# Second block's attention: two heads' scores and values on halves of TensorE, with two buffers for turned weights

## The chip, the cores and the metric

One Trainium2 chip; the kernel is one launch on one of its cores. The metric is the time of an execution in microseconds (us), the median of several runs. The core's engines are TensorE (matrix multiply; PE in profiles), ScalarE (ACT), VectorE (DVE), GpSimd (POOL) and SyncE (SP, which only issues transfers). They meet through semaphores: each engine runs its own list of instructions in order, and an instruction waits until named counters have reached a value.

## The reference, cut to what matters

A first block (two layers) and then a second block (two layers) over x of 256 tokens by 1024. A layer of the second block computes two attentions of 8 heads each, "mla" with keys of 96 features and "dilated" with keys of 64, both with values of 64:

```
for l in range(DEPTH):                       # DEPTH = 2
    h = rmsnorm(x, attn_norm[l])
    c_q, c_kv, k_r, q_d, k_d, v_d = split(h @ w_in[l])
    o_a = mla_mixer(c_q, c_kv, k_r, ...)     # 8 heads, q.k over 96, softmax, times v (64)
    o_b = dilated_attention(rmsnorm(q_d), rmsnorm(k_d), v_d, rel_bias)   # 8 heads, q.k over 64, + bias
    x = x + concat(o_a, o_b) @ w_out[l]
    x = x + conv_ffn(rmsnorm(x, ffn_norm[l]), ...)
```

Everything is float32. A head has 256 queries and 256 keys.

## The kernel before

Activations lie with features on partitions and the 256 tokens along the free axis. Weights come from HBM in pieces of at most 128 x 2048 (`raw`, three buffers) and are split into a rounded half (`wh`, made by ScalarE) and the rest (`wl`, VectorE), so that a large product is three fast float32r matmuls. The small products of attention are plain float32; each such matmul shows as two records in the trace.

A planner, `plan_program`, writes one list of steps, and each engine walks this list and issues its own part of every step. The order of the list is thus the order on every engine at once. PSUM has 8 banks, handed out in the order in which they were given back; `E2` are two buffers for a head's scores and weights, `pT2` one buffer for turned weights, `tmp` eight scratch buffers.

In a layer of the second block the order comes from generators. `mla_proj` is the list of projection work (pieces of `w_in`, the queries, four key parts, the values); `heads("d")` and `heads("m")` are the attention of the eight dilated and the eight mla heads. The dilated heads are interleaved with `mla_proj`, the mla heads with what is left of it and with half of the output projection (`dil_half`). `run_pending` issues at once what an earlier piece left to do: the norm and rotation of a head group (step `hn2`: TensorE sums of squares and a rotation by matmul, ScalarE a logarithm and an exponential, VectorE up to four products over 96 x 512), of which `queries` leaves two.

A head h goes through these steps: `sc2` (scores S: two matmuls into a bank), `exp2` (E: VectorE adds the bias for dilated heads and takes the maximum, ScalarE the exponential), `wt2` (W: VectorE divides), `turn2` (T: four transposes by TensorE, then ScalarE copies the bank to `pT`), `val2` (V: two matmuls; after every odd head ScalarE and VectorE write the pair's result as `hc_hi` and `hc_lo`). Before, the loop's turn for h is E(h+1), W(h), S(h+2), some projection work, V(h-1), T(h). Scores of an odd head use rows 64 to 127 of the array for dilated heads (rows 0 to 95 for mla heads whatever the head), and its values go to columns 64 to 127, that of an even head to 0 to 63.

In the rows below `kd,qd` are dilated scores, `k,q` mla scores, `cst,e` transposes, `pT,vd` and `pT,v` values of dilated and mla heads, `96*96 96x512` the matmuls of `hn2` for the queries, `ckn_hi,wh` key parts, `raw,csil` a product of the first block (step `mod`) in which four matmuls use four groups of 32 columns.

Of the kernel before, what the change touches and what calls it, by code (L numbers as in the profile page):

```python
# [15 lines left out]
P = 128  # L16
# [138 lines left out]
class Memory:  # L155
    def __init__(self, nc, banks):
# [219 lines left out]
def plan_program(M, pieces):  # L376
# [153 lines left out]
    def run_pending():  # L530
        while pending:
            pending.pop(0)()
# [486 lines left out]

    E2, pT2 = Bufs(M.E2), Bufs(M.pT2)  # L1020
    s = "x"
    for l in range(2):
# [90 lines left out]
        def mla_values(f):  # L1113
            for j in range(2):
# [4 lines left out]
                v_toks.append(x)  # L1119

        def mla_proj():
            for fn in (lambda: dil_piece(1), lambda: dil_piece(3), lambda: queries(0), lambda: dil_piece(5),
                       lambda: queries(1)):
                run_pending()
                tk = fn()
                if tk is not None:
                    hfree["x"] = [tk]
                yield
            f = take(("ukv", l))
            prev = None  # L1130
            for hp in range(4):
                run_pending()
# [32 lines left out]

        def heads(kind):
            mla = kind == "m"
            sc, st_, outs = {}, {}, {}
# [24 lines left out]
            def turned(h):  # L1193
                E, r = st_[h]
                b, pT = banks.get(), pT2.get()
# [4 lines left out]
                st_[h] = (pT, x)  # L1200

            def values(h):
                pT, x = st_[h]
                if h % 2 == 0:
                    outs[0] = banks.get()
                ob = outs[0]
                t = ev("mm")
                y = (ev("mx_hi"), ev("mx_lo")) if h % 2 else None
                step("val2", mla=mla, h=h, pT=pT, ready=[x, v_toks if mla else dil[4 + h // 4]], ob=ob, free=ob.free,
                     t=t, y=y, mix_free=list(hfree["c"]))  # L1210
                pT2.give(pT, t)
                if y:
                    banks.give(ob, y[1])
                    mix_toks[h // 2 + (0 if mla else 4)] = y
# [103 lines left out]
def tensor_program(pe, on, M, plan):  # L1318
# [159 lines left out]

    def sc2(mla, h, b, free, ready, t, **_):
        on.wait_ge(ready, free)  # L1480
        p0 = 64 * (h % 2)
        for qt in range(2):
            o, sl = b.t[:, T * qt:T * qt + T], slice(qt * P, qt * P + P)
            if mla:
                ins = mm(o, M.q2[:, h, sl], M.k2[:, h, :], qt == 0, True)
            else:
                ins = mm(o, M.qd[p0:p0 + 64, h // 2, sl], M.kd[p0:p0 + 64, h // 2, :], qt == 0, True)
        ins.then_inc(*on.inc(t))

# [7 lines left out]

    def val2(mla, h, pT, ready, ob, free, t, **_):
        vv, p0 = M.v2 if mla else M.vd, 64 * (h % 2)
# [11 lines left out]
def scalar_program(act, on, M, plan, io):  # L1511
# [192 lines left out]

    def val2(mla, h, ob, t, y, mix_free, **_):
        if y:
            on.wait_ge(t, mix_free)
            fn(M.H["c"][0][:, h // 2 + (0 if mla else 4), :], ob.t[:, 0:T], ACT.Copy).then_inc(*on.inc(y[0]))

# [22 lines left out]
def vector_program(dve, on, M, plan):  # L1732
# [228 lines left out]

    def val2(mla, h, ob, t, y, mix_free, **_):
        if y:
            c = h // 2 + (0 if mla else 4)
            on.wait_ge(t, y[0], mix_free)
            tt(M.H["c"][1][:, c, :], ob.t[:, 0:T], M.H["c"][0][:, c, :].bitcast(F32),
               ALU.subtract).then_inc(*on.inc(y[1]))

# [276 lines left out]
```

## Time and profile before

| | |
|---|---|
| median of 3 runs | 1796.46 us (1794.7 to 1797.76) |
| the profiled execution | 1794.97 us, its span 1793.1 us |
| TensorE busy | 1685.8 us, 94% of the span |
| VectorE, ScalarE busy | 1063.0 us (59%), 886.3 us (49%) |
| GpSimd busy | 192.7 us (11%) |
| mean granted TensorE clock | 0.977 of full |
| attention, layer 1 of the second block | 1119.2 to 1226.2 us |
| attention, layer 2 | 1483.1 to 1589.7 us |

A span is the time from the first to the last instruction. Busy shares are means over stages that have different limits; busy TensorE is not TensorE at its peak, since the ends of matmuls are modelled. A granted clock of 1.00 is 2.4 GHz, 0.50 is 1.2 GHz.

### The profile page before, as it was taken

What the parts mean: (1) busy time and instruction counts of PE and PEld (TensorE: products, weight loads), DVE (VectorE), ACT (ScalarE), POOL (GpSimd) and SP (SyncE); (2) the same over time, 40 slices, a digit from 0 to 9 for tenths busy, and PEclk for the clock granted to TensorE, in tenths of its full rate; (3) what the DMA queues carried; (4) which work ended last, traced back from release to release, by engine and by line L of the source; (5) the groups of instructions that cost most, each with busy time, mean ns of one, the idle gap of its engine ahead of it and who ended that gap; (6) DMA issues with size and microseconds to landing.
All of it is one profiled execution on the core that took longest, in us unless ns stands there. A gap on an engine that the chain in (4) does not pass through costs nothing. (4 is left out here: it accounts for less than half of the span.)

```text
span 1793.1 us, 30262 instructions
## 1 busy us (share of the span) xinstructions
PE 1685.8 (94%) x12864; PEld 1526.0 (85%) x12864; DVE 1063.0 (59%) x1472; ACT 886.3 (49%) x1192; POOL 192.7 (11%) x138
## 2 busy tenths in 40 slices
PE   5899988999999999997999999988999999889999
PEld 2777666999999999965899989757999987679999
DVE  2498657644445444986644445755776456657773
ACT  3334555544345434555544335655555366556552
POOL 1140000122003210300022100000011000000110
PEclk7899999999999999999999999999999999999999
DMA  9233646466446545363266453302555533025553
GB/s 368 94 141 136 240 165 216 184 235 252 171 165 211 185 174 182 141 238 138 99 221 201 172 174 130 132 22 86 186 184 194 177 120 134 24 95 184 184 195 119
DMA packets 45110, 299.12 MB, mean 167 GB/s; under 512 B 5216, under 2 KB 7360, under 8 KB 11696
## 3 DMA queue, kind: packets, MB, share of 16 engines
q1 hardware_dynamic: 44304, 295.65, 46.0%
q8 instruction: 102, 1.67, 0.4%
q0 software_dynamic: 240, 0.79, 0.1%
q10 hardware_dynamic: 432, 0.75, 0.1%
q14 instruction: 32, 0.26, 0.0%
HBM read 296.10 MB, written 1.06 MB: 166 GB/s over the span
## 5 line engine op out<-in xcount | busy, mean ns | idle before, releaser
L1749 DVE TENSOR_TENSOR wl<-raw,wh 128x2048 fp32r<-128x2048 f32 (+3 forms) x236 | 529.0, 2242 | 520.8 <-ACT wh L1523 470.0
L1523 ACT ACTIVATE wh<-raw 128x2048 fp32r<-128x2048 f32 (+3 forms) x236 | 436.8, 1854 | 259.4 <-PE bank L1334 158.8
L1329 PE MATMUL bank<-hx_hi,wh 128*128 128x256 f32 x1920 | 547.9, 285 | 16.3 <-ACT hx_hi L1523 9.7
L1332 PE MATMUL bank<-hx_hi,wl 128*128 128x256 f32 x1920 | 539.8, 281 | 3.3 <-DVE wl L1749 3.3
L1334 PE MATMUL bank<-hx_lo,wh 128*128 128x256 f32 x1920 | 540.4, 281 | 0.0
L1329 PEld LDWEIGHTS bank<-hx_hi,wh 128*128 128x128 f32 x1920 | 364.0, 190 | 23.9 <-issue 19.7
L1332 PEld LDWEIGHTS bank<-hx_hi,wl 128*128 128x128 f32 x1920 | 364.3, 190 | 8.8 <-DVE wl L1749 4.6
L1334 PEld LDWEIGHTS bank<-hx_lo,wh 128*128 128x128 f32 x1920 | 363.8, 189 | 0.5 <-DVE hx_lo L1741 0.2
L1332 PE MATMUL bank<-hid_hi,wl 128*128 128x256 f32 x880 | 245.4, 279 | 0.5 <-DVE wl L1749 0.5
L1334 PE MATMUL bank<-hid_lo,wh 128*128 128x256 f32 x880 | 245.4, 279 | 0.0
L1329 PE MATMUL bank<-hid_hi,wh 128*128 128x256 f32 x880 | 245.3, 279 | 0.0
L1329 PE MATMUL bank<-hc_hi,wh 128*128 128x256 f32 x752 | 218.8, 291 | 6.2 <-issue 2.7
L1332 PE MATMUL bank<-hc_hi,wl 128*128 128x256 f32 x752 | 215.2, 286 | 7.6 <-DVE wl L1749 7.6
L1334 PE MATMUL bank<-hc_lo,wh 128*128 128x256 f32 x752 | 214.6, 285 | 1.3 <-DVE hc_lo L1856 0.8
L1332 PEld LDWEIGHTS bank<-hid_hi,wl 128*128 128x128 f32 x880 | 165.2, 188 | 0.8 <-DVE wl L1749 0.8
L1334 PEld LDWEIGHTS bank<-hid_lo,wh 128*128 128x128 f32 x880 | 165.1, 188 | 0.0
L1329 PEld LDWEIGHTS bank<-hid_hi,wh 128*128 128x128 f32 x880 | 165.0, 187 | 0.0
L1329 PEld LDWEIGHTS bank<-hc_hi,wh 128*128 128x128 f32 x752 | 146.1, 194 | 19.5 <-issue 19.2
L1332 PEld LDWEIGHTS bank<-hc_hi,wl 128*128 128x128 f32 x752 | 146.1, 194 | 9.0 <-DVE wl L1749 8.6
L1334 PEld LDWEIGHTS bank<-hc_lo,wh 128*128 128x128 f32 x752 | 146.2, 194 | 2.0 <-DVE hc_lo L1856 0.9
L1523 ACT ACTIVATE tmp<-bank,vec 128x256 f32<-128x256 f32 (+3 forms) x188 | 105.8, 586 | 70.1 <-PE bank L1334 39.7
L2031 POOL TENSOR_TENSOR hid_lo<-tmp,hid_hi 128x512 fp32r<-128x512 f32 x33 | 91.7, 2779 | 349.7 <-ACT hid_hi L1523 349.7
(208 smaller groups left out, 1955.0 us busy)
## 6 DMA issues: line engine op xcount, KB each, us to landing
raw<-in_wts SPq DMA_DIRECT2D x258, 1024.0 KB, 4.8
raw<-in_wts SPq DMA_DIRECT2D x20, 768.0 KB, 4.0
raw<-in_wts SPq DMA_DIRECT2D x4, 576.0 KB, 3.5
tmp<-tscr SPq DMA_DIRECT2D x16, 128.0 KB, 4.3
raw<-in_wts SPq DMA_DIRECT2D x2, 640.0 KB, 3.9
xTc<-in_ctxT SPq DMA_DIRECT2D x1, 1024.0 KB, 10.8
xTx<-in_xT SPq DMA_DIRECT2D x1, 1024.0 KB, 8.6
out_x<-xTx POOLq DMA_DIRECT2D x3, 256.0 KB, 5.5
```

Of the source, the lines that this page charges most:

```text
L1329: pe.matmul(out, hi[:, k, c:c + m], x_hi, start=first and k == 0 and o == 0, stop=False, skip_group_check=True)
L1332: pe.matmul(out, lo[:, k, c:c + m], x_hi, start=False, stop=False, skip_group_check=True)
L1334: ins = pe.matmul(out, hi[:, k, c:c + m], x_lo, start=False, stop=last and k == nk - 1, skip_group_check=True)
L1523: return act.activation(out, in_, func, bias=bias, scale=scale)
L1749: tt(M.wl[k][:, 0:ne], M.raw[f["r"]][:, 0:ne], M.wh[k][:, 0:ne].bitcast(F32), ALU.subtract).then_inc(*on.inc(f["tlo"]))
L2031: tt(lo, y.t[:, :], hi.bitcast(F32), ALU.subtract).then_inc(*on.inc(t[1]))
```

## The change

Scores and values of heads 2u and 2u+1 become one step each. `sc2` takes two banks; for dilated heads the matmuls go even, odd, even, odd over the two halves of the rows; for mla heads the even head's two come first. `val2` writes both heads into one bank, even and odd in turns over the two halves of the columns, from two buffers `pT2` (the second one lies behind the bias table). S(u+1) now stands at the turn of the even head, V(u-1) too, so T of an even and T of an odd head follow each other with no V between. In `mla_proj` the two left-over `hn2` are issued in different turns (`one_by_one`), which makes two turns more; ten turns of the dilated loop take them all.

```
@@ heads @@
-            def scores(h):
-                b = banks.get()
-                t = ev("mm")
-                ready = (q_toks[h // 2], k_toks[h // 2]) if mla else (dil[h // 4], dil[2 + h // 4])
-                step("sc2", mla=mla, h=h, b=b, free=b.free, ready=ready, t=t)
-                sc[h] = (b, t)
+            def scores(u):
+                bs = [banks.get(), banks.get()]
+                ts = [ev("mm"), ev("mm")]
+                ready = (q_toks[u], k_toks[u]) if mla else (dil[u // 2], dil[2 + u // 2])
+                step("sc2", mla=mla, u=u, bs=bs, free=[b.free for b in bs], ready=ready, ts=ts)
...
             scores(0)
             exps(0)
-            scores(1)
             yield
             for h in range(8):
                 if h + 1 < 8:
                     exps(h + 1)
                 weights(h)
-                if h + 2 < 8:
-                    scores(h + 2)
+                if h % 2 == 0 and h < 6:
+                    scores(h // 2 + 1)
                 yield
-                if h:
-                    values(h - 1)
+                if h % 2 == 0 and h:
+                    values(h // 2 - 1)
                 turned(h)
             yield
-            values(7)
+            values(3)
@@ mla_proj @@
+        def one_by_one():
+            while pending:
+                pending.pop(0)()
+                if pending:
+                    yield
...
-                run_pending()
+                yield from one_by_one()
@@ TensorE: sc2 @@
+        for n in range(4):
+            qt, i = (n % 2, n // 2) if mla else (n // 2, n % 2)
+            o, sl, p0 = bs[i].t[:, T * qt:T * qt + T], slice(qt * P, qt * P + P), 64 * i
@@ TensorE: val2 @@
         for kt in range(2):
-            ins = mm(ob.t[p0:p0 + 64, 0:T], vv[:, kt, 64 * h:64 * h + 64], pT.t[:, kt, :], kt == 0, kt == 1)
+            for i in range(2):
+                c = 64 * (2 * u + i)
+                ins = mm(ob.t[64 * i:64 * i + 64, 0:T], vv[:, kt, c:c + 64], pT[i].t[:, kt, :], kt == 0, kt == 1)
```

On TensorE, dilated heads, behind the first product of the queries: before, T(0), S(3), the four matmuls of two `hn2`, and then the 48 of the next piece.

```order
L1494 MATMUL bank<-cst,e_0_123 128x128 x4
L1354 MATMUL bank<-kd,qd 128x256 x2
L1354 MATMUL bank<-tmp_81,cst 96x512
L1354 MATMUL bank<-tmp_85,cst 96x512
L1354 MATMUL bank<-tmp_86,cst 96x512
L1354 MATMUL bank<-tmp_84,cst 96x512
L1346 MATMUL bank<-wh_59,hx_hi 128x256
```

The same place in the changed kernel:

```order
L1500 MATMUL bank<-cst,e_0_124 128x128 x4
L1358 MATMUL bank<-tmp_81,cst 96x512
L1358 MATMUL bank<-tmp_85,cst 96x512
L1500 MATMUL bank<-cst,e_1_125 128x128 x4
L1358 MATMUL bank<-kd,qd 128x256 x4
L1358 MATMUL bank<-tmp_86,cst 96x512
L1358 MATMUL bank<-tmp_84,cst 96x512
L1350 MATMUL bank<-wh_59,hx_hi 128x256
```

T(1), which stood behind the 48 matmuls, now stands ahead of them, and the pair's scores S(4), S(5) with it.

On VectorE, dilated heads, around the second pair of `hn2` (`wl_63` is a weight piece's rest, `ropeS` begins a rotation, `e` with `bias` begins E of a head, `e_0` or `e_1` with `st` is W of an even or odd head); before, W(4) comes last:

```order
L1749 TENSOR_TENSOR wl_63<-raw_57,wh_60 128x2048
L1791 TENSOR_TENSOR tmp_81<-bank,ropeS 96x512
L1792 TENSOR_TENSOR tmp_80<-tmp_80,ropeC 96x512
L1794 TENSOR_TENSOR tmp_81<-tmp_81,tmp_80 96x512
L1796 TENSOR_TENSOR q_116<-tmp_81,tmp_85 96x512
L1791 TENSOR_TENSOR tmp_80<-bank,ropeS 96x512
L1792 TENSOR_TENSOR tmp_84<-tmp_84,ropeC 96x512
L1794 TENSOR_TENSOR tmp_80<-tmp_80,tmp_84 96x512
L1796 TENSOR_TENSOR q_116<-tmp_80,tmp_82 96x512
L1741 SCALAR_TENSOR_TENSOR e_1_124<-bank,bias 128x512
...
L1737 TENSOR_SCALAR e_0_123<-e_0_123,st_76 128x256 x2
```

The same place in the changed kernel, where W(5) comes ahead of the second rotation:

```order
L1756 TENSOR_TENSOR wl_63<-raw_57,wh_60 128x2048
L1798 TENSOR_TENSOR tmp_81<-bank,ropeS 96x512
L1799 TENSOR_TENSOR tmp_80<-tmp_80,ropeC 96x512
L1801 TENSOR_TENSOR tmp_81<-tmp_81,tmp_80 96x512
L1803 TENSOR_TENSOR q_117<-tmp_81,tmp_85 96x512
L1972 TENSOR_TENSOR hc_lo<-bank,hc_hi 128x256
L1748 SCALAR_TENSOR_TENSOR e_0_124<-bank,bias 128x512
L1956 TENSOR_REDUCE st_78<-e_0_124 128x2
L1744 TENSOR_SCALAR st_78<-st_78 128x2
L1963 RECIPROCAL st_77<-st_77 128x2
L1744 TENSOR_SCALAR e_1_125<-e_1_125,st_77 128x256 x2
L1798 TENSOR_TENSOR tmp_80<-bank,ropeS 96x512
```

One rotation, the pair's `hc_lo` and E(6) stand ahead of W(5); W(4) has moved ahead of the weight piece.

On TensorE, last mla heads, before: V and T in turns.

```order
L1354 MATMUL bank<-pT_0_125,v_118 64x256 x2
L1494 MATMUL bank<-cst,e_0_123 128x128 x4
L1354 MATMUL bank<-pT_0_125,v_118 64x256 x2
L1494 MATMUL bank<-cst,e_1_124 128x128 x4
L1354 MATMUL bank<-pT_0_125,v_118 64x256 x2
```

The same place in the changed kernel, with the pair's values in turns over two buffers:

```order
L1358 MATMUL bank<-pT_0_126,v_119 64x256
L1358 MATMUL bank<-pT_1_112,v_119 64x256
L1358 MATMUL bank<-pT_0_126,v_119 64x256
L1358 MATMUL bank<-pT_1_112,v_119 64x256
L1500 MATMUL bank<-cst,e_0_124 128x128 x4
L1500 MATMUL bank<-cst,e_1_125 128x128 x4
L1358 MATMUL bank<-pT_0_126,v_119 64x256
```

V of both heads is one run of matmuls, and T of the odd head follows T of the even one.

## Rows read from the trace of the kernel before

**Rows 1.** The page: the span, and TensorE's line of its first part

```profile
span 1793.1 us, 30262 instructions
PE 1685.8 (94%) x12864; PEld 1526.0 (85%) x12864; DVE 1063.0 (59%) x1472; ACT 886.3 (49%) x1192; POOL 192.7 (11%) x138
```

**Rows 2.** Busy time by stretches: us, engines busy (x instructions), PEclk, DMA share, GB/s

```profile
1119.20:1165.70 46.50, 46.18 (x273) 34.33 (x272) 32.18 (x51) 31.07 (x56) 0.00 (x0) 1.00 0.38 135
1165.70:1184.70 19.00, 13.38 (x51) 8.02 (x51) 10.00 (x26) 8.86 (x23) 0.00 (x0) 0.82 0.01 1
1184.70:1226.20 41.50, 37.12 (x224) 28.11 (x223) 22.46 (x52) 22.43 (x54) 0.00 (x0) 1.00 0.15 52
...
1529.60:1547.20 17.60, 11.75 (x51) 7.13 (x50) 10.03 (x26) 8.75 (x23) 0.00 (x0) 0.90 0.00 1
1547.20:1589.70 42.50, 38.62 (x224) 29.61 (x223) 22.54 (x52) 22.73 (x54) 0.00 (x0) 0.96 0.14 50
...
1169.20:1176.10 6.90, 6.90 (x20) 4.58 (x21) 3.93 (x9) 4.18 (x11) 0.00 (x0) 0.51 0.01 4
```

**Rows 3.** TensorE's waits, attention of layer 1: us in total, times, longest

```profile
PE bank L1494 <- DVE e L1737: 4.2, 3, 2.9
PE bank L1354 <- ACT pT L1523: 4.1, 6, 0.7
PE bank L1354 <- DVE k L1939: 1.7, 1, 1.7
```

**Rows 4.** Timeline, TensorE: start, us, instruction, xrecords; scores and column groups

```profile
215.83 1.07 PE L1354 MATMUL bank<-raw,csil 128*32 128x512 f32 x8
...
1119.15 1.14 PE L1354 MATMUL bank<-kd,qd 64*128 64x256 f32 x8
...
1126.93 1.13 PE L1354 MATMUL bank<-kd,qd 64*128 64x256 f32 x4
...
1184.64 1.99 PE L1354 MATMUL bank<-k,q 96*128 96x256 f32 x8
1186.47 1.02 PE L1354 MATMUL bank<-tmp,cst 96*96 96x512 f32 x2
```

**Rows 5.** Timeline, TensorE: values, transposes and the waits ahead of them

```profile
1133.07 0.60 PE L1494 MATMUL bank<-cst,e 128*128 128x128 f32 x4
...
1134.66 3.67 PE L1354 MATMUL bank<-tmp,cst 96*96 96x512 f32 x8
...
1143.92 1.08 PE L1354 MATMUL bank<-pT,vd 128*64 128x256 f32 x4
1144.93 0.66 PE L1494 MATMUL bank<-cst,e 128*128 128x128 f32 x4
...
1168.54 0.66 PE L1494 MATMUL bank<-cst,e 128*128 128x128 f32 x4 [2.86 <-DVE e L1737]
...
1225.12 1.08 PE L1354 MATMUL bank<-pT,v 128*64 128x256 f32 x4 [0.69 <-ACT pT L1523]
```

**Rows 6.** Timeline, VectorE: what stands ahead of W(1) and of W(4)

```profile
1136.64 0.61 DVE L1737 TENSOR_SCALAR e<-e,st 128x256 f32<-128x256 f32 x2
...
1158.67 2.29 DVE L1749 TENSOR_TENSOR wl<-raw,wh 128x2048 fp32r<-128x2048 f32 x1 [2.38 <-ACT wh L1523]
1160.88 0.68 DVE L1791 TENSOR_TENSOR tmp<-bank,ropeS 96x512 f32<-96x512 f32 x1
...
1163.52 0.68 DVE L1791 TENSOR_TENSOR tmp<-bank,ropeS 96x512 f32<-96x512 f32 x1
...
1166.16 0.68 DVE L1741 SCALAR_TENSOR_TENSOR e<-bank,bias 128x512 f32<-128x512 f32 x1
1166.88 0.69 DVE L1949 TENSOR_REDUCE st<-e 128x2 f32<-128x512 f32 x1
...
1167.87 0.61 DVE L1737 TENSOR_SCALAR e<-e,st 128x256 f32<-128x256 f32 x2
1170.29 0.42 DVE L1966 TENSOR_TENSOR hc_lo<-bank,hc_hi 128x256 fp32r<-128x256 f32 x1 [1.81 <-ACT hc_hi L1523]
```

**Rows 7.** ScalarE's groups, attention of layer 1: busy us, mean ns | idle before

```profile
L1523 ACT ACTIVATE wh<-raw 128x2048 fp32r<-128x2048 f32 x7 | 13.3, 1905 | 0.0
L1523 ACT ACTIVATE pT<-bank 128x512 f32<-128x512 f32 x16 | 9.5, 594 | 6.7 <-PE bank L1494 6.7
...
L1523 ACT ACTIVATE hc_hi<-bank 128x256 fp32r<-128x256 f32 x8 | 3.0, 380 | 8.1 <-PE bank L1354 8.1
```

More of the change, by code:

```diff
@@ L1018, in store @@
         step("store", ch=ch, ready=t, t=ev("out", 16) if ch < 3 else ev("out_end", 16))
-    E2, pT2 = Bufs(M.E2), Bufs(M.pT2)
+    E2, pT2 = Bufs(M.E2), [Buf(t) for t in M.pT2]
     s = "x"
@@ L1131, in mla_proj @@
             for hp in range(4):
-                run_pending()
+                yield from one_by_one()
                 if prev:
@@ L1194, in turned @@
                 E, r = st_[h]
-                b, pT = banks.get(), pT2.get()
+                b, pT = banks.get(), pT2[h % 2]
                 t, x = ev("mm"), ev("pT")
@@ L1199, in turned, with values @@
                 banks.give(b, x)
[L1200 to L1214, printed above, removed]
+                st_[h] = x
+            def values(u):
+                ob, t, y = banks.get(), ev("mm"), (ev("mx_hi"), ev("mx_lo"))
+                step("val2", mla=mla, u=u, pT=pT2, ready=[st_[2 * u], st_[2 * u + 1], v_toks if mla else dil[4 + u // 2]],
+                     ob=ob, free=ob.free, t=t, y=y, mix_free=list(hfree["c"]))
+                for pT in pT2:
+                    pT.free = [t]
+                banks.give(ob, y[1])
+                mix_toks[u + (0 if mla else 4)] = y
             scores(0)
             exps(0)
-            scores(1)
             yield
@@ L1477, in mla_k2, with sc2 @@
         mm(nb.t[0:96, :], M.ones[0:96, 0:96], sq.t[0:96, :], True, True).then_inc(*on.inc(tn))
[L1479 to L1483, printed above, removed]
+    def sc2(mla, u, bs, free, ready, ts, **_):
+        on.wait_ge(ready, free[0])
+        for n in range(4):
+            qt, i = (n % 2, n // 2) if mla else (n // 2, n % 2)
+            o, sl, p0 = bs[i].t[:, T * qt:T * qt + T], slice(qt * P, qt * P + P), 64 * i
+            on.wait_ge(free[i])
             if mla:
-                ins = mm(o, M.q2[:, h, sl], M.k2[:, h, :], qt == 0, True)
+                ins = mm(o, M.q2[:, 2 * u + i, sl], M.k2[:, 2 * u + i, :], qt == 0, True)
             else:
-                ins = mm(o, M.qd[p0:p0 + 64, h // 2, sl], M.kd[p0:p0 + 64, h // 2, :], qt == 0, True)
-        ins.then_inc(*on.inc(t))
+                ins = mm(o, M.qd[p0:p0 + 64, u, sl], M.kd[p0:p0 + 64, u, :], qt == 0, True)
+            if qt:
+                ins.then_inc(*on.inc(ts[i]))
     def turn2(E, r, b, free, t, **_):
@@ L1496, in turn2, with val2 @@
         ins.then_inc(*on.inc(t))
-    def val2(mla, h, pT, ready, ob, free, t, **_):
-        vv, p0 = M.v2 if mla else M.vd, 64 * (h % 2)
+    def val2(mla, u, pT, ready, ob, free, t, **_):
+        vv = M.v2 if mla else M.vd
         on.wait_ge(ready, free)
         for kt in range(2):
-            ins = mm(ob.t[p0:p0 + 64, 0:T], vv[:, kt, 64 * h:64 * h + 64], pT.t[:, kt, :], kt == 0, kt == 1)
+            for i in range(2):
+                c = 64 * (2 * u + i)
+                ins = mm(ob.t[64 * i:64 * i + 64, 0:T], vv[:, kt, c:c + 64], pT[i].t[:, kt, :], kt == 0, kt == 1)
         ins.then_inc(*on.inc(t))
@@ L1703, in turn2, with val2 @@
         fn(pT.t[:, :, :].rearrange("p a t -> p (a t)"), b.t[:, :], ACT.Copy).then_inc(*on.inc(x))
[L1705 to L1708, printed above, removed]
+    def val2(mla, u, ob, t, y, mix_free, **_):
+        on.wait_ge(t, mix_free)
+        fn(M.H["c"][0][:, u + (0 if mla else 4), :], ob.t[:, 0:T], ACT.Copy).then_inc(*on.inc(y[0]))
     def tconv(l, i, g, b, tk, y, free, t_a, **_):
@@ L1960, in wt2, with val2 @@
             ts(e, e, d.t[:, 6 + qt:7 + qt], ALU.mult).then_inc(*on.inc(t_w[1 + qt]))
[L1962 to L1967, printed above, removed]
+    def val2(mla, u, ob, t, y, mix_free, **_):
+        c = u + (0 if mla else 4)
+        on.wait_ge(t, y[0], mix_free)
+        tt(M.H["c"][1][:, c, :], ob.t[:, 0:T], M.H["c"][0][:, c, :].bitcast(F32),
+           ALU.subtract).then_inc(*on.inc(y[1]))
     def tconv(l, i, g, b, y, t_a, t_c, **_):
```

6 lines of the change are left out of this document (4 added, 2 removed).

## The prediction

> **What bounds the kernel now.** I read the page first: TensorE is busy for 1685.8 of 1793.1 us [rows 1], so time taken off TensorE is time off the kernel wherever nothing else ends last. Whether that holds in the second block's attention I read from the busy times by stretches. The dilated loop up to 1165.7 is TensorE's: 46.18 of 46.50 us [rows 2]. Then come 19.0 us (17.6 in layer 2) in which it works for only 13.4, and the mla loop of 41.5 us (42.5 in layer 2) with 37 to 39 of work. The waits of that attention are few and have three releasers: the last product of W on VectorE (4.2 us), ScalarE's copy of turned weights (4.1) and once VectorE's keys (1.7) [rows 3]. In the middle stretch the granted clock also fell: 0.51 (the 1.2 GHz level) from 1169.2 to 1176.1, directly behind the wait of 2.86 ahead of T(4) [rows 2, 5]. So the question is how much of the saved TensorE work lies where TensorE ends last.
>
> **What the change takes off TensorE.** The trace already has a pair: the dilated scores of heads 0 and 1 stand next to each other on the two halves of the rows, and their eight records take 1.14 us, while one head's four take 1.13 [rows 4]. Halves of rows run at the same time. Three more pairs per layer, at about 1.06, give 3.2 us. The mla scores use 96 rows and gain nothing (eight records 1.99) [rows 4]. Halves of columns do not occur, but quarters do: eight records with 32 columns each take 1.07, where two passes over 512 columns last 1.02 and eight would take about four times that [rows 4]. Groups of columns run together too. A head's V then costs 1.01 (start to start) [rows 5], and eight of sixteen per layer vanish: 8.1. Together 11.3 per layer, 22.6 for both, so 1794.97 - 22.6 = 1772.4 if all of it arrived. If column halves did not overlap, V would stay as it is.
>
> **Why most of the dilated part does not arrive.** I walked layer 1 with the new order, each instruction at its duration of before.
> - T(0) is unchanged at 1133.1 [rows 5]. T(1) used to stand behind the next weight piece; now only two of the four matmul pairs of `hn2` (half of 3.67, 1.8 us [rows 5]) lie between. T(0) and these are over at 1133.07 + 0.60 + 1.84 = 1135.5, with the changes of tile near 1135.8, but W(1) ends at 1136.64 + 0.61 = 1137.25 [rows 6]. A new wait of 1.5. Behind it stands the whole in-order list of TensorE: S(4), S(5) and the next 48 matmuls, which start near 1140.6; before they followed the 3.67 that begin at 1134.66, near 1138 [rows 5]. The 2.6 later are the wait, T(1) and more changes of tile.
> - T(4) then comes at about 1157.9, with a wait of some 0.8 for W(4).
> - Between there and T(5) VectorE has a serial chain. ScalarE's split (1905 ns [rows 7]) of the piece is pushed behind E(5), to 1160.1; VectorE's `wl` (2.29), which waits for it today too (2.38), ends at 1162.4 and not at 1160.9 [rows 6]. Then a rotation (1163.52 - 1160.88 = 2.64), a `hc_lo` of about 0.4, and E(6) with W(5), 1167.87 + 0.61 - 1166.16 = 2.3 [rows 6]: T(5) at 1167.7.
> - TensorE is out of work earlier than before. It stood idle from 1168.54 - 2.86 = 1165.7 [rows 5]; three score pairs (3.2) and two value pairs (2.0) are gone, the waits of 1.5 and 0.8 came in: by the list 1162.6. The wait ahead of T(5) is then **5.1 us** instead of 2.86. The saving has become a wait for VectorE.
> - Behind T(5) VectorE has the second rotation (2.64) and again E, W (2.3): T(6) at 1172.7. TensorE fills this with the values' projection (3.0). Then a key part, T(7), a copy (0.59 [rows 7]) and V: the mla scores start at about 1178.1 instead of 1184.64 [rows 4]. That is 6.5 earlier in layer 1, 5.1 in layer 2, whose stretch was 1.4 shorter (17.6 against 19.0 [rows 2]). This takes both at the full clock.
>
> Much of the 6.5 is therefore no saved matmul at all: it is the time that before lost at the half clock and that TensorE spent on work which now fits into the wait.
>
> **The mla part.** V gives 4.1 per layer. Against it stands that W(odd) can no longer hide behind V(even - 1): V is over, then VectorE writes `hc_lo` behind ScalarE's `hc_hi` (0.38 + 0.42 [rows 6, 7]), the maximum (0.69), and W (0.17 + 0.61) [rows 6] before T(odd); 2.5 together, of which T(even) covers 0.6. So 1.9 ahead of T(3) and of T(5), about 1.6 ahead of T(1), 1.05 ahead of T(7), 1.7 ahead of S (keys, as before [rows 3]), and twice a copy of 0.7: 9.8 with small ones. Before, 1.7, three of the six copies (2.1) and half of the 1.3 that e has besides its 2.9 stood there [rows 3]: 4.4. The walked list is 42.95 long at the full clock (nearly 41.5 - 4.1 + 5.4), against 41.5 in layer 1 and 42.5 in layer 2, where a part was at a lower clock, 0.96 [rows 2]: +1.45 + 0.45 = **+1.9**.
>
> The Trainium skill, "TensorEngine Tiling (Array Packing)", sections Theoretical Speedup and PSUM Bottleneck, promises up to 2x for dimensions of 64 and warns that this speeds TensorE but not the emptying of PSUM. By the first alone all 22.6 would arrive; by the second little. The rows of waits above side with the second.
>
> **The clock.** In the trace the clock fell to 0.51 behind a wait of 2.86 [rows 2, 5]. I expect it again behind the wait of 5.1: the three microseconds of projection matmuls there take twice as long (+3.0), of which 0.5 is hidden in the wait for W(6): +2.5 per layer, **+5.0**. And once more in the mla loop, whose waits are now 1.6 to 1.9, in one of the two layers: I price it at **+2.4**, the size of the first. An exclusion of either I cannot get from the trace; the bounds are 0 and about 12.5 (each of two layers twice, plus one).
>
> The Trainium skill, "TensorE: Matmul & The Clock Gate", section Why this matters for your kernels, says that idle gaps between bursts of matmuls bring the clock back to half. It speaks against this change, which makes gaps longer; without it, by the rows of waits alone, the time would be 1786.8 (B below).
>
> **The sum.** -6.5 - 5.1 + 1.9 + 5.0 + 2.4 = -2.3, against the profiled execution's own 1794.97: 1792.7. The median of the runs lies 1.5 above that execution: 1794.2. I round towards a slightly smaller second drop and say 1793.5, 0.16% under the median. A difference under 0.2% (3.6 us: 1792.9 to 1800.0) is about what a measurement of this kernel cannot tell from no change.
>
> **Rivals.**
> - **A, the gain turns into waits on VectorE's chain, with one half-clock stretch per layer or a little more** (above): 0.50. Its own range is 1790 to 1798.
> - **B, the same without new half-clock stretches.** -6.5 - 5.1 + 1.9 = -9.7: 1786.8. For it: in layer 2 the present stretch had 0.90, not 0.82 [rows 2], so the drop is not certain behind a gap. Against: the gaps are longer. 0.20. More of the saving (towards 1774) would need VectorE's chain to be shorter than its rows.
> - **C, slower: the clock falls in the mla loop too.** Place: T(3), T(5), with waits near 1.9 twice in some ten microseconds and then the output projection. Each half-clock stretch like that of 1169.2 to 1176.1 (6.9 us at 0.51) costs up to 3.4 [rows 2]. From two per layer beyond A's on it decides: -9.7 + 5.0 + 4 x 3 = +7, to about 1801 to 1804. Against: waits of 0.69 and 1.7 did not drop it in layer 1 (1.00 over 41.5 us [rows 2]). 0.17.
> - **D, halves of columns do not overlap as alternated here.** V then keeps its 1.01 per head: +4.0 per layer in the mla part, and part of it in the dilated one, whose wait hides the rest: 1793.5 + 12 to 14 = about 1807. For it: only quarters are in the trace. Against: these quarters, and halves of rows. 0.05.
> - **E, nothing visible:** the wait ahead of T(5) grows by all that TensorE saves, and the tail behind it does not shorten. Time 1796.5. 0.08.
>
> **How the numbers follow.** Faster by over 0.2%: B's 0.20, and somewhat under half of A, 0.20: 0.40. Slower: 0.17 of C and D's 0.05, of which a little is within 0.2%, 0.20. Same: 0.40. For 8 in 10, the range leaves out the lower part of B and D with the upper part of C: 1786 to 1802.
>
> **What the profile after would show.** Right: eight records of pT,vd and of pT,v in about 1.1 us (1.0 per head would be D); four times eight records kd,qd in 1.1; a wait of 1.5 ahead of T(1), and one of about 5 ahead of T(5), released by VectorE's e; mla scores of layer 1 starting near 1178 (B) or 1180.6 (A); waits near 1.9 for e ahead of T(3) and T(5) in the mla part; a stretch at 0.5 behind the wait of 5. Wrong if: ScalarE's split is not late, so that the wait ahead of T(5) stays near 3 (then up to 2 per layer more is gained); the mla waits stay under 1; or half-clock stretches appear in the mla loop (C).

## The result

The changed kernel takes 1803.39 us (1798.76 to 1805.3), the kernel before, run beside it, 1797.74 us (1794.7 to 1800.54), eight runs each: ratio 1.0026, 95% interval 1.0014 to 1.0038. It is slower by 0.26%, just above the range that was given.

The page of the changed kernel, its span and TensorE's line, for [rows 1]:

```profile
span 1803.5 us, 30274 instructions
PE 1677.4 (93%) x12864; PEld 1524.4 (85%) x12864; DVE 1062.9 (59%) x1472; ACT 887.0 (49%) x1192; POOL 192.8 (11%) x138
```

TensorE is busy for 8.4 us less and the span is 10.4 us longer. Part of that is chance: the profiled execution is the changed kernel's slowest of eight, and that of before is near its fastest. Laying the two traces side by side, matmul by matmul, the changed one is 2.0 us late already when the dilated loop begins (1121.16 instead of 1119.15), though no instruction differs up to there. It gathers 4.0 us more in the last feed-forward part. There the granted clock is 1.00 in both, but over most of it TensorE starts 90 or 91 matmuls in 10 us before and 87 in the changed kernel, of the same products; nothing in the traces says why. Between these, the shift goes from 2.0 to 3.8 over the first attention, from 3.6 to 4.9 over the second, and to 6.4 within 20 us behind it.

Of these shifts the four loops of the two attentions give 3.2 us, and they belong to the change. The last 1.5 is one stretch at half clock behind the layer 2 attention. It stands behind two waits for ScalarE (0.96 and 2.07 us) that every kernel here has, and the kernel before has such a stretch behind layer 1 and none behind layer 2, so it cannot be put down to the change. Together they are 4.7, of which the stretch between the layers gives 0.3 back; the medians are 5.65 apart.

Busy time by stretches for the changed kernel, columns as in [rows 2]: dilated and mla loop of layer 1, the same of layer 2 (a dilated loop here begins with the first `kd,qd` and ends with the first `k,q`; an mla loop ends with the last `pT,v`), and four pieces of layer 1:

```profile
1121.16:1181.69 60.53, 51.28 (x324) 38.42 (x323) 41.99 (x76) 40.04 (x79) 0.00 (x0) 0.94 0.29 104
1181.69:1230.05 48.36, 39.01 (x225) 29.86 (x223) 22.54 (x52) 22.43 (x54) 0.00 (x0) 0.86 0.12 44
1486.63:1547.05 60.42, 51.12 (x324) 38.26 (x323) 42.00 (x76) 40.02 (x79) 0.00 (x0) 0.94 0.30 105
1547.05:1594.70 47.65, 37.84 (x225) 29.26 (x223) 22.53 (x52) 22.44 (x54) 0.00 (x0) 0.89 0.13 45
1169.70:1175.50 5.80, 5.80 (x16) 4.49 (x16) 4.60 (x10) 4.11 (x11) 0.00 (x0) 0.53 0.00 0
1187.70:1193.70 6.00, 6.00 (x25) 4.40 (x26) 1.66 (x6) 2.41 (x7) 0.00 (x0) 0.72 0.00 0
1209.60:1213.00 3.40, 3.40 (x15) 3.04 (x14) 0.86 (x1) 2.43 (x5) 0.00 (x0) 0.55 0.12 51
1222.70:1233.00 10.30, 8.89 (x38) 6.09 (x39) 2.18 (x7) 4.51 (x9) 0.00 (x0) 0.51 0.01 2
```

Before, the dilated loops took 65.5 and 64.1 us, the mla loops 41.6 and 42.6 (between the same matmuls). So the dilated loops gain 5.0 and 3.7 us, and the mla loops lose 6.8 and 5.1. In layer 1 the clock of the mla loop was 1.00 before [rows 2] and is now 0.86; it falls three times, the last time into the output projection. In layer 2 it falls three times as well (0.89).

The waits of TensorE in that attention, for [rows 3], and its timeline (start, us, instruction, xrecords, wait and releaser), for [rows 4, 5]:

```profile
PE bank L1500 <- DVE e L1744: 13.4, 7, 5.3
PE bank L1358 <- ACT pT L1531: 2.3, 3, 0.8
PE bank L1358 <- DVE k L1946: 1.7, 1, 1.7
```

```profile
1139.33 0.66 PE L1500 MATMUL bank<-cst,e 128*128 128x128 f32 x4 [1.26 <-DVE e L1744]
1139.91 1.13 PE L1358 MATMUL bank<-kd,qd 64*128 64x256 f32 x8
...
1157.72 1.08 PE L1358 MATMUL bank<-pT,vd 128*64 128x256 f32 x8
1159.78 0.66 PE L1500 MATMUL bank<-cst,e 128*128 128x128 f32 x4 [0.97 <-DVE e L1744]
...
1169.65 1.12 PE L1500 MATMUL bank<-cst,e 128*128 128x128 f32 x4 [5.35 <-DVE e L1744]
...
1187.64 2.73 PE L1358 MATMUL bank<-k,q 96*128 96x256 f32 x8 [1.74 <-DVE k L1946]
...
1204.41 1.08 PE L1358 MATMUL bank<-pT,v 128*64 128x256 f32 x8
1205.43 0.65 PE L1500 MATMUL bank<-cst,e 128*128 128x128 f32 x4
1208.03 0.66 PE L1500 MATMUL bank<-cst,e 128*128 128x128 f32 x4 [1.95 <-DVE e L1744]
1208.52 2.92 PE L1358 MATMUL bank<-k,q 96*128 96x256 f32 x8
```

Halves of the columns do run together: eight records of `pT,vd` or `pT,v` in 1.08 us, where one head's four took 1.08. But the waits for VectorE's `e` have grown from 4.2 to 13.4 us. The same eight `k,q` that took 1.99 take 2.73 and 2.92 where the clock has fallen behind such a wait.

### The profile page after: what moved, and what is told of

Its sections match the earlier page's. It is cut to its first block and busy times, and to the rows that moved or that the text cites. A ratio compares the mean times of both kernels' runs of the same rounds, so it can differ in the third digit from the quotient of the medians.

```text
span 1803.5 us, 30274 instructions
## 1 busy us (share of the span) xinstructions
PE 1677.4 (93%) x12864; PEld 1524.4 (85%) x12864; DVE 1062.9 (59%) x1472; ACT 887.0 (49%) x1192; POOL 192.8 (11%) x138
```

## The experiments

The theory after the result: the dilated pairs gain what their loops show, the mla pairs lose more than that, through waits of T(odd) for W(odd) and, above all, through the clock that falls behind them. The rivals: the attention parts cancel and the difference stands outside (N); or the waits count and not the clock. Loop lengths below are of layer 1 / layer 2, cut as above; ratios are to the kernel before, run beside each group of kernels. In the kernels of this section `sc2` and `val2` take a list of heads, one or two, and can be set by kind; `hc_hi`, `hc_lo` are a step of their own (`mix2`), which stands where `val2` had it unless said otherwise.

| run | what differs from the kernel before | ratio, 95% | dilated loops | mla loops |
|---|---|---|---|---|
| the change | all | 1.0026 (1.0014 to 1.0038) | 60.5 / 60.4 | 48.4 / 47.7 |
| e1 | dilated pairs, norms in turns | 0.9947 (0.9934 to 0.9959) | 60.5 / 60.5 | 42.6 / 42.6 |
| e2 | mla pairs | 1.0049 (1.0035 to 1.0062) | 65.5 / 65.5 | 46.6 / 45.8 |
| e3 | the change, late hc | 0.9964 (0.995 to 0.9977) | 60.3 / 59.7 | 43.4 / 41.8 |
| e4 | the change, mla waits filled | 0.9969 (0.9956 to 0.9983) | 59.6 / 60.6 | 43.3 / 43.7 |
| e5 | dilated scores in pairs, norms in turns | 0.9957 (0.9943 to 0.9971) | 61.8 / 60.6 | 41.6 / 41.6 |
| e6 | e1, mla values in pairs, late hc | 0.9948 (0.9936 to 0.996) | 60.2 / 59.7 | 40.5 / 40.4 |
| e8 | e3, waits of both loops filled | 0.9953 (0.9941 to 0.9965) | 59.7 / 59.7 | 41.4 / 41.4 |
| e10 | e3, W ahead of E | 1.0086 (1.0066 to 1.0106) | 64.3 / 64.3 | 46.9 / 46.9 |
| e12 | norms in turns, no pairs | 0.9948 (0.9931 to 0.9965) | 59.8 / 60.6 | 41.6 / 41.6 |
| e13 | dilated pairs, norms as before | 0.9998 (0.9986 to 1.0009) | 63.4 / 63.3 | 43.6 / 43.5 |
| e14 | e6, waits of both loops filled | 0.9916 (0.9896 to 0.9936) | 59.7 / 59.7 | 39.9 / 39.9 |
| e15 | e1, heads ahead of the projection | 0.9972 (0.9956 to 0.9988) | cut elsewhere | 41.6 / 41.6 |
| f1 | e12, mla scores in pairs | 0.9968 (0.9953 to 0.9982) | 59.8 / 59.8 | 44.4 / 43.6 |
| f2 | e12, mla values in pairs | 0.9962 (0.9949 to 0.9975) | 60.7 / 60.6 | 41.2 / 41.2 |
| f3 | e12, mla values in pairs, late hc, mla waits filled | 0.9933 (0.9914 to 0.9952) | 59.8 / 59.8 | 39.9 / 39.9 |

Two lengths of one and the same loop differ by up to 1.5 us, by where the clock happened to fall: 65.5 and 64.1 for the dilated loop of the kernel before, 43.4 and 41.8 for the mla loop of e3. The stretch ahead of the first attention, with the same instructions in all but e15, took between 1116.6 and 1126.2 us in the profiled executions. So the loops tell more than the whole, and a difference between two loops is safe where both have the clock at 1.00.

**Which loop loses: e1 and e2.** The pairs by kind; `ps` and `pv` say whether this kind's scores and values go in pairs. In e1 they hold for "d" alone, in e2 for "m" alone (and there `run_pending` stands in place of `one_by_one`).

```
-            scores(0)
+            scores([0, 1] if ps else [0])
             exps(0)
+            if not ps:
+                scores([1])
...
-                if h % 2 == 0 and h < 6:
-                    scores(h // 2 + 1)
+                if ps:
+                    if h % 2 == 0 and h < 6:
+                        scores([h + 2, h + 3])
+                elif h + 2 < 8:
+                    scores([h + 2])
                 yield
-                if h % 2 == 0 and h:
-                    values(h // 2 - 1)
+                if pv:
+                    if h % 2 == 0 and h:
+                        values([h - 2, h - 1])
+                elif h:
+                    values([h - 1])
                 turned(h)
```

> Pairs for the dilated heads alone; the mla heads go one by one in the order of before. Theory M (the dilated pairs gain 5.0 and 3.7 us, as the two traces show between the same matmuls, and the mla pairs lose more than that): about 1797.7 - 8.7 = 1789, ratio to before near 0.995, and the mla loops about 41.5 us long with the 0.69 waits of before. Theory N (the parts of the attention nearly cancel by chance and the measured 0.26% stands for places outside it, as the 2.0 us ahead of the attention and 2.7 us in the last feed-forward of the one profile): ratio within 0.998 to 1.002.

> Pairs for the mla heads alone; the dilated heads and the left-over norms as before. Theory M: mla loop some 6.8 and 4.9 us longer than before's 41.5 and 42.5, with half-clock stretches behind it: 1797.7 + 13 = about 1810, ratio 1.006 to 1.008. Theory N: ratio within 0.999 to 1.003.

e1 took 1788.59 us, 0.53% under before; e2 1807.15 us, 0.49% over. Theory N falls: the change is the sum of a gain of about 9 us and a loss of more. But the two halves alone add up to about nothing (-0.53% and +0.49%), and the change to +0.26%; e2's loss is also smaller than Theory M had it (1.006 to 1.008). The mla loops show the rest. In e2 they are 1.7 and 1.8 us shorter than in the change, and in e1, whose mla heads are those of before, they are 42.6 and not the 41.5 expected, with the clock at 0.96: it falls once per loop, behind the wait for the keys.

**hc ahead of W, and the clock: e3 and e4.** e3 issues `mix2` behind W of the next turn:

```
                 weights(h)
+                while mixes:
+                    mixes.pop()()
```

> The changed kernel, but the pair's hc_hi and hc_lo are a step of their own that stands behind W of the next odd head, on ScalarE and VectorE; TensorE's order is the same. Prediction's mechanism (T(3) and T(5) of the mla loop wait 1.95 each because VectorE has hc_lo, the maximum and W ahead of it): both waits go to nearly nothing. If only the waits count: 1803.4 - 4 x 1.9 = 1795.8. If the half clock behind them goes too (two of the three half-clock stretches per mla loop): 5 to 7 us less again, 1789 to 1791. Rival (V's own end, not hc_lo, is what W waits for, or ScalarE's copies come late instead): waits of over 1 us stay in these places and the time is 1800 or more.

e4 leaves the order alone and gives TensorE matmuls that nobody reads in its mla waits:

```
+    def filler(key, b, free):
+        n = FILL.get(key, 0)
+        if n:
+            on.wait_ge(free)
+        for _ in range(n):
+            mm(b.t[:, 0:P], M.ones, M.ones, True, True)
...
     def turn2(mla, h, E, r, b, free, t, **_):
+        filler(("m" if mla else "d", "T", h), b, free)
         on.wait_ge(r, free)
```

> The changed kernel with matmuls that nobody reads (128 columns, into a bank that is written over later) issued in the waits of the mla loop: 5 ahead of T(1), 7 ahead of S(2), 8 ahead of T(3) and of T(5), 2 ahead of T(7), 3 ahead of V(4) and V(6). The waits' ends stay where they are, only TensorE's idling is gone. If the half clock in the mla loop is due to that idling: clock there 1.00 and 4 to 5 us less per layer, 1793 to 1796. If the clock falls for another reason (half-used rows or columns in the pairs) or its fall costs nothing: 1802 to 1806.

e4 is the cleanest result of all: 1791.97 us, ratio 0.9969 where the change has 1.0026. The order is that of the change, with matmuls without a reader added, and 0.57% went: some 10 us, give or take 3 by the two intervals. Its stretches, mla loops of layers 1 and 2:

```profile
1183.68:1227.02 43.34, 41.29 (x296) 35.00 (x296) 22.54 (x52) 22.42 (x54) 0.00 (x0) 1.00 0.14 49
...
1544.34:1588.03 43.69, 41.30 (x296) 35.02 (x296) 22.54 (x52) 22.42 (x55) 0.00 (x0) 1.00 0.14 49
```

The clock is 1.00 (2.4 GHz) throughout. Of the 6.8 and 5.1 us that the mla loops lose, the clock is 5.0 and 4.0; the waits themselves are the other 1.8 and 1.1 (in layer 2 against a loop that itself had a stretch at half clock, 0.96). The pairs' half-used rows or columns do not lower the clock by themselves.

The 1.95 ahead of T(3) is what VectorE does behind V; the changed kernel's VectorE there, then that of e3:

```profile
1206.03 0.42 DVE L1972 TENSOR_TENSOR hc_lo<-bank,hc_hi 128x256 fp32r<-128x256 f32 x1
1206.37 0.68 DVE L1956 TENSOR_REDUCE st<-bank 128x2 f32<-128x512 f32 x1
...
1207.36 0.62 DVE L1744 TENSOR_SCALAR e<-e,st 128x256 f32<-128x256 f32 x2
```

```profile
1199.21 2.29 DVE L1817 TENSOR_TENSOR wl<-raw,wh 128x2048 fp32r<-128x2048 f32 x1 [2.29 <-issue]
1201.42 0.68 DVE L2017 TENSOR_REDUCE st<-bank 128x2 f32<-128x512 f32 x1
...
1202.41 0.62 DVE L1805 TENSOR_SCALAR e<-e,st 128x256 f32<-128x256 f32 x2
1203.80 0.42 DVE L2033 TENSOR_TENSOR hc_lo<-bank,hc_hi 128x256 fp32r<-128x256 f32 x1 [0.78 <-PE bank L1560]
```

With `hc_lo` behind W the wait is 1.23 ahead of T(3) and 0.78 ahead of T(5), not nothing. Ahead of T(3) the weight piece's `wl` (2.29) still stands before the maximum and W. Ahead of T(5) VectorE is no longer late: ScalarE's copy of T(4) releases it (`ACT pT`). e3 took 1791.08 us (0.9964), the second of the two sums expected, but with only half of these waits gone and less of the half clock (0.92 and 0.96 in the mla loops, against 0.86 and 0.89).

**The dilated values: e5.** Only the dilated scores in pairs (`pv` false for both kinds).

> Only the dilated scores in pairs (and the left-over norms in different turns); values one head at a time, mla heads as before. Against the run with dilated pairs of both kinds (0.9947) it tells what the dilated values are worth. Prediction's step (VectorE's chain ahead of T(5) fixes that point, so V saved before it only lengthens the wait): the wait ahead of T(5) is about 2 us shorter than 5.4 and the time only the two V pairs behind T(5) higher, 2 us per layer: 1792 to 1794, ratio 0.997. Rival (TensorE's time counts as a whole): 4 us per layer higher, 1796 to 1797, ratio 0.9995.

1788.19 us, 0.9957. Its wait ahead of T(5) is 3.48 instead of 5.40 in e1, as foreseen, but both expected times were too high (1792 to 1794, and 1796 to 1797): the dilated loops are only 1.3 and 0.1 us longer than in e1, and the mla loops 1.0 shorter each, at a clock of 1.00. Eight values per layer in pairs are worth at most 1.3 us in the dilated loop, of the 4.1 that they take off TensorE; even the two pairs behind T(5), for which 2 us per layer were expected, give no more.

**Mla values with single scores: e6.** e1 with `pv` for both kinds and late hc.

> Dilated pairs as changed; of the mla heads only the values in pairs, their scores one head at a time as before, and hc_hi, hc_lo behind W of the odd head. If the mla values can be had once the scores stay single: loop 40 to 41 us instead of 42.6, ratio 0.992 to 0.993. Rival (T of the odd head still has nothing to stand behind; about 1.2 ahead of T(3) and 0.8 ahead of T(5) as in the run with late hc, and the half clock with it): loop 42.5 or more, ratio 0.995.

The loops did go to 40.5 and 40.4, the first theory's length, yet the whole is 0.9948, not to be told from e1, and the expected ratio was not met. In the profiled executions e6's four loops are 5.4 us shorter than e1's, and the stretches behind them, whose instructions do not differ, take 4.0 of that back. First e1, then e6, between the layers and behind layer 2:

```profile
1220.69:1476.01 255.32, 248.74 (x2053) 245.24 (x2053) 164.15 (x206) 137.85 (x164) 19.06 (x18) 0.99 0.47 165
1579.09:1786.50 207.41, 201.04 (x1690) 199.81 (x1690) 132.31 (x166) 102.93 (x116) 18.36 (x17) 1.00 0.45 158
```

```profile
1220.15:1476.96 256.81, 250.22 (x2053) 246.66 (x2053) 164.18 (x206) 138.02 (x164) 19.09 (x18) 0.99 0.47 164
1577.00:1786.90 209.90, 203.48 (x1691) 202.25 (x1690) 132.32 (x166) 103.09 (x116) 18.36 (x17) 0.99 0.45 156
```

Behind both mla loops of e6 the clock falls to half once more, at the waits of 0.96 and 2.07 for ScalarE that also stood in the result; in e1 it falls behind neither. That the other executions of e6 did the same is not shown, though their mean granted clock points that way: 0.975 to 0.979, e1's 0.977 to 0.979, where e6's loops alone have the higher clock.

**The clock in the dilated part: e8.** e3 with fillers in both loops (`FILL` has 20 ahead of the dilated T(5)).

> The run with late hc, and matmuls that nobody reads in the waits of both loops: 20 ahead of the dilated T(5), 5 ahead of the dilated T(1), in the mla loop 7 ahead of S(2), 5, 5, 3, 2 ahead of T(1), T(3), T(5), T(7), 3 ahead of V(4) and V(6). If the half clock after the 5 us wait costs what the prediction said (2.5 per layer), and that after the keys' wait and at the end about 3 per layer more: 1791.1 - 11 = 1780, ratio 0.990, with a granted clock of 1.00 through both layers. Rival (the time at half clock is hidden behind VectorE's chain, so that T(6) and the mla loop start no earlier): 1788 to 1791, ratio 0.995.

1787.62 us, 0.9953: not 0.990. TensorE of e8, the dilated T(5) to V(7); the first row is the matmuls without a reader:

```profile
1161.93 4.73 PE L1404 MATMUL bank<-cst 128*128 128x128 f32 x40 [0.73 <-DVE tmp L1859]
1166.50 0.60 PE L1560 MATMUL bank<-cst,e 128*128 128x128 f32 x4
...
1172.30 0.66 PE L1560 MATMUL bank<-cst,e 128*128 128x128 f32 x4 [1.39 <-DVE e L1805]
...
1176.72 1.08 PE L1404 MATMUL bank<-pT,vd 128*64 128x256 f32 x8 [1.05 <-ACT pT L1592]
```

The clock is 1.00 and the values follow T(5) after 3.3 us instead of 5.9 in e3, but now T(6) waits 1.39 for VectorE and V(7) 1.05 instead of 0.77. The dilated loops are 59.7, against 60.3 and 59.7 of e3. The rival is right for this loop: the half clock behind the long wait is nearly all hidden under VectorE's chain. In the mla loop it was not hidden.

**Another order of E and W: e10.**

```
+                weights(h)
                 if h + 1 < 8:
                     exps(h + 1)
-                weights(h)
```

> The run with late hc, and in each turn W of head h ahead of E of head h + 1 on both engines. VectorE's chain ahead of T(5) in the dilated part is 1.5 us shorter (bias and maximum of E(6) gone from it), those ahead of T(3) and T(5) in the mla loop 0.9 us. If these chains set the starts: wait ahead of T(5) near 3.6, T(3) and T(5) of the mla loop under 0.5, ratio 0.993 to 0.994. Rival (E comes later in its place and the wait moves to the next T): sum of waits on e unchanged near 9.7, ratio 0.996 or above.

1811.84 us, 1.0086, worse than any other. The wait ahead of T(5) fell from 5.07 in e3 to 2.95, as the chain says, but the next maximum and exponential came late, and with them ScalarE's work for the norms. TensorE of e10:

```profile
1156.90 3.42 PE L1404 MATMUL bank<-tmp,cst 96*96 96x512 f32 x4 [3.01 <-ACT tmp L1592]
...
1169.81 0.66 PE L1560 MATMUL bank<-cst,e 128*128 128x128 f32 x4 [2.95 <-DVE e L1805]
...
1183.27 1.08 PE L1404 MATMUL bank<-pT,vd 128*64 128x256 f32 x8 [2.44 <-ACT pT L1592]
```

The rival was right in kind, the wait moves, and too mild in size.

**Pairs or order in the dilated loop: e12 and e13.** e12 has `ps` and `pv` false for both kinds and keeps `one_by_one`; e13 is e1 with `run_pending`:

```
         def mla_proj():
...
-                yield from one_by_one()
+                run_pending()
```

> No pairs at all: scores, values and mla heads one by one as before; only the left-over norms (hn2) are issued in different turns, as in the change, with two buffers for turned weights. If the pairs carry the 5 and 4 us that the dilated loops gain: ratio within 0.998 to 1.001. Rival (the gain comes from the new order, because W(5) no longer stands behind both rotations on VectorE, and overlap adds little): dilated loops 62 to 63 us instead of 65.5 and 64.1, ratio 0.996 to 0.998.

> The run with dilated pairs and mla heads as before, but the two left-over norms are issued at once as before. If the pairs' TensorE time is what counts: dilated loops 61 to 62 us, ratio 0.995 to 0.997. Rival (the order of the norms carries the gain: with both rotations ahead of an odd head's W on VectorE the wait grows by a rotation, 2.6 us): dilated loops 63 us or more, ratio 0.998 to 1.000.

This turned the account of the gain over. e12 has not one pair more than before and takes 1787.47 us (0.9948), as little as e1, and less than even its rival had (0.996 to 0.998); e13 has the dilated pairs and takes 1796.46 us (0.9998), as its rival said. The second buffer for turned weights is not the cause either: e2 has it with the norms as before, and its dilated loops are 65.5 us long. Loop by loop e12 is even the shorter of the two: its four loops are 2.7 us shorter than e1's in the profiled executions, and e1 has it back behind them, where its clock did not fall (see e6). Stretches of e12, dilated and mla loop of layer 1, and its TensorE and VectorE around T(5):

```profile
1117.79:1177.59 59.80, 56.18 (x324) 40.21 (x322) 41.99 (x76) 39.67 (x79) 0.00 (x0) 1.00 0.30 105
1177.59:1219.15 41.56, 37.18 (x223) 28.10 (x222) 22.45 (x52) 22.41 (x54) 0.00 (x0) 1.00 0.15 51
```

```profile
1166.58 0.66 PE L1560 MATMUL bank<-cst,e 128*128 128x128 f32 x4 [2.51 <-DVE e L1805]
1169.97 1.08 PE L1404 MATMUL bank<-pT,vd 128*64 128x256 f32 x4
1171.46 0.66 PE L1560 MATMUL bank<-cst,e 128*128 128x128 f32 x4 [0.42 <-DVE e L1805]
```

```profile
1159.02 2.29 DVE L1817 TENSOR_TENSOR wl<-raw,wh 128x2048 fp32r<-128x2048 f32 x1 [2.37 <-ACT wh L1592]
1161.23 0.68 DVE L1859 TENSOR_TENSOR tmp<-bank,ropeS 96x512 f32<-96x512 f32 x1
...
1165.91 0.61 DVE L1805 TENSOR_SCALAR e<-e,st 128x256 f32<-128x256 f32 x2
1166.44 0.68 DVE L1859 TENSOR_TENSOR tmp<-bank,ropeS 96x512 f32<-96x512 f32 x1
```

W(5) at 1165.91 stands between the two rotations (1161.23 and 1166.44), where before both stood ahead of E and W [rows 6]. T(5) waits 2.51; the next T waits 0.42, and the clock stays at 1.00, so that the loop has 56.18 us of TensorE work in 59.80 us. (In layer 2 the clock did fall behind the same wait, 0.97 over the loop, and it is 60.6 long.) In e1 it has 51.19 in 60.49: 5.0 us of work less, and it ends no earlier. What fixes the end is VectorE's chain: T(5) starts 48.5 us into the loop in e1 and in e5, and 48.7 in e12, with all, half or none of the pairs.

In e13 the waits of the attention of layer 1 are 5.2 for `e` (5 times), 4.8 for `pT` and 1.3 for a rotation's `tmp`, in the dilated loop above all, and the clock of that loop is 0.90.

**Filled and without the scores' pairs: e14.** e6 with fillers.

> Dilated pairs, mla values in pairs, mla scores single, late hc, and matmuls that nobody reads in the waits: 7 ahead of the mla S(2), 4 ahead of T(3), 3 ahead of V(4) and V(6), 16 ahead of the dilated T(5), 5 ahead of the dilated T(1). The best that these parts give together: the half clock behind the keys' wait goes (1.5 us of the 40.5 of the loop), dilated loop 59.7: ratio 0.993 to 0.994. Rival (nothing left to gain, the other waits take it): ratio 0.9945 to 0.995.

1781.46 us, 0.9916 (0.9896 to 0.9936): the best version found, below e1 and below both kernels, and a little better than expected (0.993 to 0.994). The mla loop of layer 1 takes 39.86 us at a clock of 1.00. Against e6 the four loops are only 1.7 us shorter; in its profiled execution the clock also fell behind neither mla loop (255.2 and 207.4 us there, against e6's 256.8 and 209.9).

**The heads first: e15.** In each turn `next(gd)` stands ahead of `next(gp)`.

> Dilated pairs, mla heads as before, and in each turn of the dilated loop the head's steps ahead of the projection's on all engines, so that W(5) stands ahead of the last split and of the rotation on VectorE. If that chain sets the end of the dilated loop: wait ahead of T(5) under 3, loop 58 to 59 us, ratio 0.992 to 0.993. Rival (what is put behind, the split and the norms, is needed next, and the wait moves to the projection): loop 61 us or more, ratio 0.996 or above.

1791.33 us, 0.9972, worse than e1, as the rival said. Its first dilated scores now wait for the norm of the keys (2.74, released by VectorE's `kd`), and T(4) and T(5) still wait up to 2.7. This loop begins one piece of projection earlier in the list, so its length does not compare.

**Which mla pairing loses: f1 to f3.** All on e12; f1 pairs the mla scores, f2 the mla values, f3 the values with late hc and fillers.

> The run without pairs but with the norms in different turns (ratio 0.9948, mla loops 41.5), and the mla scores alone in pairs. If the mla loss comes from the values' pairing (T of the odd head behind nothing, hc_lo ahead of W): loop 41.5 to 42.5, ratio 0.995 to 0.996. Rival (the pair of scores takes from T(odd) the score that stood ahead of it and hid W, so it loses by itself): loop 43 to 44, with waits for e ahead of the mla T(odd) of 1 us or more and a half-clock stretch, ratio 0.997 to 0.999.

> The same base, the mla values alone in pairs, hc_hi and hc_lo ahead of W of the odd head as in the change. If it is this pairing that loses: loop 44 us or more, ratio 0.998 or above. If single scores cover W: loop 40 to 42, ratio 0.993 to 0.995.

> The same base, mla values in pairs with late hc, and unread matmuls: 7 ahead of the mla S(2), 4 ahead of T(3), 3 ahead of V(4) and V(6). The earlier run with these and with dilated pairs gave 0.9916. If the dilated pairs are worth nothing, as the run without pairs says: 0.991 to 0.993, loops 39.9. Rival (they were worth something there, since the clock was kept): 0.994 or above.

TensorE of f1, then of f2, around T(2) and T(3) of the mla loop:

```profile
1202.77 0.66 PE L1560 MATMUL bank<-cst,e 128*128 128x128 f32 x4
1204.11 1.08 PE L1404 MATMUL bank<-pT,v 128*64 128x256 f32 x4 [0.69 <-ACT pT L1592]
1205.36 0.66 PE L1560 MATMUL bank<-cst,e 128*128 128x128 f32 x4 [0.17 <-DVE e L1805]
```

```profile
1207.55 0.66 PE L1560 MATMUL bank<-cst,e 128*128 128x128 f32 x4
1208.05 1.03 PE L1404 MATMUL bank<-k,q 96*128 96x256 f32 x4
1210.64 0.66 PE L1560 MATMUL bank<-cst,e 128*128 128x128 f32 x4 [1.57 <-DVE e L1805]
```

f1 (0.9968) loses 2.9 and 2.1 us per loop although nothing waits long: the single score that covered ScalarE's copy of pT is gone (0.69 more, twice), and in layer 1 the pair `k,q` behind the keys' wait runs at the lower clock; in layer 2 the clock stays at 1.00, so 2.1 is the price without it. f1's rival was right about the length and wrong about the place of the wait. f2 (0.9962) neither gains nor loses in its loops, 41.2 against 41.6: it has 4.0 us of TensorE work less, and its waits for `e` grow from 0.6 to 4.8, of which a single score still covers a part ahead of T(3). Its ratio stayed above the one expected (0.993 to 0.995). Each pairing alone costs nothing or 2 to 3 us per loop; both together leave T(odd) nothing at all to stand behind, and cost 3 to 5 (e2) or 5 to 7 (the change). f3 (0.9933) has the loops of e14 to 0.1 us, 59.8 without and 59.7 with the dilated pairs at a clock of 1.00; the two ratios' intervals overlap, so the dilated pairs add nothing that can be measured. The mla values in pairs, late hc and filled waits together do shorten the mla loop: 39.9 against 41.6 in e12.

## Why the prediction was wrong

**Right, part by part.** The column halves overlap, as it said. The walk of the new order holds too: 1.26 and 0.43 ahead of T(1) for a forecast 1.5; 0.97 ahead of T(4) for 0.8; 5.35 ahead of T(5) for 5.1. T(5) came at 1169.65, which less the 2.0 us of late start is 1167.6, for 1167.7. In the mla loop the waits ahead of T(3) and T(5) are 1.95 each for 1.9, that ahead of T(1) 1.28 for 1.6, and without the half clock the loop is 43.3 and 43.7 long (e4) for 42.95. The chain of `hc_lo`, maximum and W that was named is the one in the trace, and e3 confirmed it by moving it.

**The step that failed: the clock in the mla loop.** The prediction priced it "once more in the mla loop, whose waits are now 1.6 to 1.9, in one of the two layers", at +2.4. It fell three times in each layer, behind the keys' wait, behind T(3) and behind T(5), and its removal by unread matmuls gave 5.0 and 4.0 us in the loops, 9.0 where the sum has 2.4, and some 10 us in the whole. That is rival C, whose mechanism was right, with two of its three places, and which had 0.17 and about 1801 to 1804 us. Against it the prediction set that the mla loop of before kept 1.00 through waits of 0.69 and 1.7 in layer 1. Its own rows had the counter-example: in layer 2 the same loop has 0.96 [rows 2], because there the clock fell behind the same wait of 1.69.

**The clock in the dilated part was over-priced.** "+2.5 per layer": the stretch at half clock is there (0.53 from 1169.70 to 1175.50), but e8 shows that it costs 0.6 per layer at most against e3, since T(6) waits for VectorE anyhow. The same idea that explained the lost TensorE time, a late VectorE, should have been applied to the lost clock too.

**The account in numbers.** Dilated loops: forecast -6.5 - 5.1 + 5.0 = -6.6, measured -5.0 - 3.7 = -8.7. Mla loops: forecast +1.9 + 2.4 = +4.3, measured +6.8 + 5.1 = +11.9. Behind the second: 0 and +1.5, the stretch at half clock that may be chance; between the layers 0 and -0.3. Together -2.3 and +4.4. Without the clock the mla loops would be +2.9 (e4), for a forecast +1.9.

**Right number, wrong owner.** The prediction put the earlier start of the mla loop down to the pairs and the better fit of the waits. e12 and e13 show that it belongs to the norms issued in different turns: without pairs the gain is whole, with pairs and the old order it is nearly gone (2.1 and 0.8 us of loop left, and 2.1 and 0.9 lost again in the mla loop). The walk contained this (W(5) ahead of the second rotation) but it was never costed alone.

The Trainium skill's "TensorEngine Tiling (Array Packing)", section PSUM Bottleneck, warns that tiling does not speed the emptying of PSUM. The case agrees in kind, with a chain on VectorE of which emptying banks is a part: 5.0 us less work in e1's loop than in e12's, and no earlier end (60.49 against 59.80). The Trainium skill's "TensorE: Matmul & The Clock Gate", section Why this matters for your kernels, says that idle gaps between matmul bursts bring the clock back to half; e4, in which the gaps alone were filled, agrees with 0.57%.

**Open.** What decides behind which of the same waits the clock falls, and whether the dilated pairs are worth anything in the whole when the waits are filled (e14 against f3, 0.9916 and 0.9933).

## What to carry to other kernels

Work taken off an engine that is 94% busy was worth nothing that could be measured in the dilated loop, where another engine's chain set the start of T(5). So cost each part of a change alone, the reordering above all, for here a change of order without a pair gave all of the gain. Before two steps are joined, ask what stood between them and whose latency it hid. And where short waits gather, look at the clock: matmuls that nobody reads, issued in those waits, gave back 0.57% here. And where a wait left the clock alone in one layer, look at the other layers before counting on it.

## What the runs showed of the hardware

The two halves of the columns, issued in turns into one bank, take 1.08 us for eight records, what four take.

A clock fall does not go with the length of one wait alone: the keys' wait of 1.7 us left 1.00 in the mla loop of layer 1 of the kernel before and of e12, and was followed by slower `k,q` in the changed kernel, in e3 and in f1 (2.73, 2.66 and 2.31 us for the eight that take 1.99). It is not the order alone either: in e3's layer 2 the same `k,q` behind the same wait of 1.69 took 2.00. The waits of 0.96 and 2.07 some 15 us behind each mla loop are the same in all seventeen profiled executions, and the clock fell to half behind them in ten of the seventeen in layer 1 and in eleven in layer 2. Such a fall costs about 1.5 us: the stretch between the layers takes 256.8 with it (e6) and 255.3 without (e1).
